# Stick-breaking attention: one split running sum instead of a separate sum of later blocks

## The reference, cut to what matters

```python
def stick_breaking(q, k, v, bias, qpos):
    kpos = jnp.arange(k.shape[1])
    z = (jnp.einsum('bqhd,bkhd->bhqk', q, k).astype(jnp.float32) * SB_SCALE
         + bias.astype(jnp.float32)[None, :, None, None])
    mask = kpos[None, :] < qpos[:, None]
    log_rest = jnp.where(mask, jax.nn.log_sigmoid(-z), 0.0)
    after = lax.cumsum(log_rest, axis=3, reverse=True) - log_rest
    a = jnp.where(mask, jnp.exp(jax.nn.log_sigmoid(z) + after), 0.0)
    return jnp.einsum('bhqk,bkhd->bqhd', a.astype(v.dtype), v)
```

## Time and profile before

| | us |
|---|---|
| median of 3 executions (1914.3 to 1914.96) | 1914.41 |
| the profiled execution | 1914.85 |
| its span, from first to last instruction | 1913.0 |
| TensorE busy | 1847.1 |
| VectorE busy | 834.4 |
| ScalarE busy | 542.8 |
| GpSimd busy | 305.3 |

### The profile page before, as it was taken

How to read it: one execution, slowest core, us unless ns; L and a number is a source line. 1 busy time by engine, 2 the same in 40 slices (tenths; PEclk the granted TensorE clock), 3 DMA queues, 4 the chain that set the end, 5 groups by cost and what they waited for, 6 DMA issues and landing times.

```text
span 1913.0 us, 28812 instructions
## 1 busy us (share of the span) xinstructions
PE 1847.1 (97%) x11073; PEld 1734.6 (91%) x11073; DVE 834.4 (44%) x1064; ACT 542.8 (28%) x871; POOL 305.3 (16%) x323
## 2 busy tenths in 40 slices
PE   6999999999899999999999989999999999999997
PEld 6878686968769989999999969999999999999996
DVE  5564737375812132232233385443124442344436
ACT  5564737372100010000022453332023220132213
POOL 1121313132501131111110121100001001010012
PEclk9999999999899999999999999999999999999998
DMA  5202030303331111111114031111111111111302
GB/s 162 67 24 66 1 88 0 87 2 110 105 115 44 40 43 38 55 50 39 49 51 143 23 112 55 44 45 54 44 44 44 47 45 48 47 44 45 135 29 94
DMA packets 162280, 113.69 MB, mean 59 GB/s; under 512 B 5389, under 2 KB 152213, under 8 KB 161947
## 3 DMA queue, kind: packets, MB, share of 16 engines
q1 hardware_dynamic: 161035, 108.34, 19.0%
q10 hardware_dynamic: 1200, 4.75, 0.7%
HBM read 95.86 MB, written 13.40 MB: 57 GB/s over the span
## 4 chain that ended last, share of the span: by engine, by line
PE 81%; DVE 11%; issue 3%; POOL 2%; ACT 2%; DMA 1%; SPq 0%; DVEq 0%; POOLq 0%; ACTq 0%
PE ps L1423 65%; PE ps L1433 8%; DVE zl L1105 2%; PE misc L1514 2%; POOL sp_hi L591 2%; PE misc L1409 1%; PE ps L1686 1%; PE ps L1504 1%; DVE kq L1145 1%; DVE later L1122 1%; DVE later L1118 1%; DVE sp_lo L1127 1%; DVE w_lo L1027 1%; DVE z_dec L1147 1%; PE ps L1499 1%
## 5 line engine op out<-in xcount | busy, mean ns | idle before, releaser
L1027 DVE TENSOR_TENSOR w_lo<-stage,w_hi 128x1024 fp32r<-128x1024 f32 x148 | 185.4, 1253 | 590.1 <-POOL w_hi L547 589.8
L1423 PE MATMUL ps<-h_hi,w_lo 128*128 128x344 f32 x1896 | 404.4, 322 | 0.0
L1423 PE MATMUL ps<-h_lo,w_hi 128*128 128x344 f32 x1896 | 403.2, 321 | 0.0
L1423 PE MATMUL ps<-h_hi,w_hi 128*128 128x344 f32 x1896 | 401.1, 320 | 0.0
L547 POOL TENSOR_SCALAR w_hi<-stage 128x1024 fp32r<-128x1024 f32 x148 | 158.0, 1068 | 1259.4 <-PE ps L1423 1097.4
L1423 PEld LDWEIGHTS ps<-h_lo,w_hi 128*128 128x128 f32 x1896 | 321.6, 189 | 0.0
L1423 PEld LDWEIGHTS ps<-h_hi,w_lo 128*128 128x128 f32 x1896 | 319.7, 188 | 1.8 <-issue 1.4
L1423 PEld LDWEIGHTS ps<-h_hi,w_hi 128*128 128x128 f32 x1896 | 316.7, 188 | 0.0
L1433 PE MATMUL ps<-h_hi,w_lo 128*128 128x344 f32 x408 | 147.7, 362 | 0.4 <-DVE w_lo L1027 0.4
L950 ACT ACTIVATE up<-ps 128x1032 f32<-128x1032 f32 x44 | 45.6, 1035 | 354.7 <-PE ps L1423 353.0
L1433 PE MATMUL ps<-h_hi,w_hi 128*128 128x344 f32 x408 | 134.5, 330 | 0.0
(11 more groups left out here) (257 smaller groups left out, 2558.3 us busy)
## 6 DMA issues: line engine op xcount, KB each, us to landing
stage<-in_w_in SPq DMA_DIRECT2D x48, 512.0 KB, 3.9
stage<-in_w_up SPq DMA_DIRECT2D x44, 512.0 KB, 3.8
stage<-in_w_down SPq DMA_DIRECT2D x16, 448.0 KB, 3.3
stage<-in_w_branch SPq DMA_DIRECT2D x24, 256.0 KB, 2.7
x_scratch<-trunk SPq DMA_DIRECT2D x1, 4128.0 KB, 13.9
x_back<-x_scratch SPq DMA_DIRECT2D x1, 4128.0 KB, 13.3
x_tok<-in_x_prompt SPq DMA_DIRECT2D x8, 512.0 KB, 8.4
kv_pg<-in_cache_k SPq DMA_DIRECT2D x16, 256.0 KB, 3.4
```

The lines of the kernel that those rows point to most:

```text
L1027: V.tensor_tensor(w_lo[par][:, :, :], stage[par][:, :, :], w_hi[par][:, :, :].bitcast(F32), ALU.subtract).then_inc(w_lo_made, 1)
L1423: last = M(ps[par][:, c, :], w[par][:, k, :], x[:, c * CH:(c + 1) * CH], start=(k == 0 and s == 0), stop=(k == n - 1 and s == 2))
```

## The change

For each chunk, own block and later blocks are now one running sum `sums` (softplus plus bias of this chunk, added to the sum of the chunk before). It is split into s_hi and s_lo. The sum within a block still takes neg_tri, now times the running sum of this chunk; the later blocks take `neg_rest`, which is minus one just where neg_tri is zero, times the running sum of the chunk before, as two float32r products. So GpSimd's high half waits for `sums_made` and not for `spn_ready`, every chunk has a sum (the `last` ones too), and the low half is a plain subtraction. ScalarE does abs, exp and ln of chunk c together, and its abs waits for the low half of chunk c - 4. The copies out of PSUM stand behind the low half of chunks 5, 13 and 22. GpSimd makes one more mask at the start, and the sample group's sums have one more product.

```diff
         ones = sb("ones", [P, P])
-        neg_ones = sb("neg_ones", [P, P])
         neg_tri = sb("neg_tri", [P, P], F32R)
+        neg_rest = sb("neg_rest", [P, P], F32R)
...
-        sp_hi = [sb(f"sp_hi{i}", [P, HALF], F32R, s_att) for i in range(3)]
-        sp_lo = [sb(f"sp_lo{i}", [P, HALF], F32R, s_att) for i in range(3)]
-        later = [sb(f"later{i}", [P, HALF], F32, s_att) for i in range(4)]
+        sums = [sb(f"sums{i}", [P, HALF], F32, s_att) for i in range(2)]
+        s_hi = [sb(f"s_hi{i}", [P, HALF], F32R, s_att) for i in range(4)]
+        s_lo = [sb(f"s_lo{i}", [P, HALF], F32R, s_att) for i in range(4)]
...
-            pool.wait_ge(consts, NCONST + 1)
+            pool.wait_ge(consts, NCONST + 3)
+            nc.gpsimd.affine_select(out=neg_rest[:, :], in_=neg_rest[:, :], compare_op=ALU.is_ge, fill=0.0,
+                                    base=-1, pattern=[[1, P]], channel_multiplier=-1).then_inc(consts, 1)
...
-                    pool.wait_ge(spn_ready, p * NCK + (c + 1))
+                    pool.wait_ge(sums_made, p * NSUMS + sums_upto[c + 1])
                     pool.wait_ge(cum_ready, p * NCK + (c + 1))
                     pool.sem_inc(hi_begun, 1)
-                    nc.gpsimd.tensor_scalar(sp_hi[c % 3][:, 0:W], zl[c % 4][:, 0:W], bias_p[:, hh:hh + 1], 1.0,
-                                            ALU.add, ALU.mult).then_inc(hi_ready, 1)
+                    nc.gpsimd.tensor_scalar(s_hi[c % 4][:, 0:W], sums[c % 2][:, 0:W], 1.0, 0.0,
+                                            ALU.mult, ALU.add).then_inc(hi_ready, 1)
...
                     act.wait_ge(z_ready, p * NCK + (c + 1))
-                    act.wait_ge(sp_ready, p * NCK + (c + 1))
+                    if c >= 4:
+                        act.wait_ge(sp_ready, p * NCK + c)
...
                     if c < NCK:
                         soft_abs(c)
-                    if 0 < c <= NCK:
-                        soft_ln(c - 1)
-                    if c < NCK:
                         soft_exp(c)
+                        soft_ln(c)
...
+                    t = zl[c % 4][:, 0:W]
+                    dve.wait_ge(l_ready, p * NCK + (c + 1))
+
+                    V.scalar_tensor_tensor(t, z_bank[c][:, 0:W], nbias_p[:, hh:hh + 1], t, ALU.max, ALU.add
+                                           ).then_inc(spn_ready, 1)
+
+                    dve.wait_ge(spn_ready, p * NCK + (c + 1))
+                    total = sums[c % 2]
+                    Wb = 0 if top else CHUNKS[c - 1][3]
+                    if Wb:
+                        dve.wait_ge(sums_made, p * NSUMS + sums_upto[c])
+                        V.scalar_tensor_tensor(total[:, W - Wb:W], t[:, W - Wb:W], bias_p[:, hh:hh + 1],
+                                               sums[(c - 1) % 2][:, 0:Wb], ALU.add, ALU.add).then_inc(sums_made, 1)
+                    if Wb < W:
+                        V.scalar_tensor_tensor(total[:, 0:W - Wb], t[:, 0:W - Wb], bias_p[:, hh:hh + 1],
+                                               ones[:, 0:W - Wb], ALU.add, ALU.mult).then_inc(sums_made, 1)
+                    dve.wait_ge(cum_ready, p * NCK + (c + 1))
+                    dve.wait_ge(hi_ready, p * NCK + (c + 1))
+                    V.tensor_tensor(s_lo[c % 4][:, 0:W], total[:, 0:W], s_hi[c % 4][:, 0:W].bitcast(F32),
+                                    ALU.subtract).then_inc(sp_ready, 1)
                     for j, (_, end) in enumerate(A_STEPS):
-                        if c == end - 1:
+                        if c == end:
...
-                    M(z, neg_tri[:, :], sp_lo[c % 3][:, 0:W], start=False, stop=False, skip_group_check=True)
-                    t = M(z, neg_tri[:, :], sp_hi[c % 3][:, 0:W], start=False, stop=top, skip_group_check=True)
+                    M(z, neg_tri[:, :], s_lo[c % 4][:, 0:W], start=False, stop=False, skip_group_check=True)
+                    t = M(z, neg_tri[:, :], s_hi[c % 4][:, 0:W], start=False, stop=top, skip_group_check=True)
                     if not top:
                         Wb = CHUNKS[c - 1][3]
-                        pe.wait_ge(later_ready, p * NLATER + later_upto[c])
-                        t = M(z[:, W - Wb:W], neg_ones[:, :], later[(c - 1) % 4][:, 0:Wb], start=False, stop=True,
+                        M(z[:, W - Wb:W], neg_rest[:, :], s_lo[(c - 1) % 4][:, 0:Wb], start=False, stop=False,
+                          skip_group_check=True)
+                        t = M(z[:, W - Wb:W], neg_rest[:, :], s_hi[(c - 1) % 4][:, 0:Wb], start=False, stop=True,
                               skip_group_check=True)
```

More of the change, by code:

```diff
@@ L112, in build @@
     NCK = len(CHUNKS)
[L114 to L118, removed]
+    sums_upto = [0]
+    for n, (_, _, _, W, top, _) in enumerate(CHUNKS):
+        sums_upto.append(sums_upto[-1] + 1 + (not top and W > CHUNKS[n - 1][3]))
+    NSUMS = sums_upto[NCK]
     SEGMENT_ENDS = [n for n, chunk in enumerate(CHUNKS) if chunk[5]]
@@ L320, in build @@
             ktok_ps, ktok_made, vtok_ps, vtok_made, small_ps, small_made, tok_out, z_ready,
-            abs_made, e_made, l_ready, spat_biased, q_pads, spn_ready, hi_ready, sp_ready, later_ready, cum_ready,
+            abs_made, e_made, l_ready, spat_biased, q_pads, spn_ready, hi_ready, sp_ready, sums_made, cum_ready,
             att_ready, pv_done, yc_hi_made, yc_made, pad_zero, own_mask, own_made, dec_o_ps, xg_ps,
@@ L336, in build @@
             "small_ps", "small_made", "tok_out", "z_ready", "abs_made", "e_made", "l_ready", "spat_biased", "q_pads",
-            "spn_ready", "hi_ready", "sp_ready", "later_ready", "cum_ready", "att_ready", "pv_done",
+            "spn_ready", "hi_ready", "sp_ready", "sums_made", "cum_ready", "att_ready", "pv_done",
             "yc_hi_made", "yc_made", "pad_zero", "own_mask", "own_made", "dec_o_ps", "xg_ps",
@@ L557, in _ @@
             nc.gpsimd.memset(ones[:, :], 1.0).then_inc(consts, 1)
-            nc.gpsimd.memset(neg_ones[:, :], -1.0).then_inc(consts, 1)
+            nc.gpsimd.memset(neg_rest[:, :].bitcast(F32), -1.0).then_inc(consts, 1)
             nc.gpsimd.memset(mask_b[:, :], NEG).then_inc(consts, 1)
@@ L565, in _ @@
                                     base=0, pattern=[[-1, P]], channel_multiplier=1).then_inc(consts, 1)
-            nc.gpsimd.affine_select(out=neg_tri[:, :], in_=neg_ones[:, :], compare_op=ALU.is_ge, fill=0.0,
+            nc.gpsimd.affine_select(out=neg_tri[:, :], in_=neg_rest[:, :], compare_op=ALU.is_ge, fill=0.0,
                                     base=0, pattern=[[-1, P]], channel_multiplier=1).then_inc(consts, 1)
@@ L662, in _ @@
             act.dma_start(g_pre[:, :], norm_mix_pre[0, :].partition_broadcast(P)).then_inc(gpre_in, 16)
-            act.wait_ge(consts, NCONST + 4)
+            act.wait_ge(consts, NCONST + 5)
             for b in range(len(IN_BATCHES) + 1):
@@ L1074, in _ @@
                 dve.wait_ge(biasp_made, p * 2 + 2)
-                nl = 0
                 def segment_lo(n):
@@ L1101, in _ @@
                                 V.tensor_copy(a_tail[:, :], last_cols(1, PTAIL)).then_inc(tail_cols, 1)
[L1102 to L1130, removed]
                 segment_lo(NSEG - 2)
@@ L1177, in _ @@
             V.tensor_tensor(zf, dec_sums, zf, ALU.add).then_inc(dec_arg, 1)
-            dve.wait_ge(consts, NCONST + 4)
+            dve.wait_ge(consts, NCONST + 5)
             V.tensor_reduce(pick[:, :], ident[0:NS * H, 0:NS * H].rearrange("p (h b) -> p b h", h=H), AX_X, ALU.add
@@ L1438, in _ @@
             ys = [(y_hi[:, k, :], y_lo[:, k, :]) for k in range(BT)]
-            pe.wait_ge(consts, NCONST + 4)
+            pe.wait_ge(consts, NCONST + 5)
             FIRST_Q = {4: (0, 0, KT), 5: (0, KT, KT), 6: (0, 2 * KT, KT),
@@ L1629, in _ @@
             M(dec_sums, neg_tri[:, :].bitcast(F32), sp_d, start=True, stop=False, skip_group_check=True)
-            M(dec_sums[:, 0:half], neg_ones[:, :], sp_d[:, half:], start=False, stop=True, skip_group_check=True
-              ).then_inc(dec_cum, 1)
+            M(dec_sums[:, 0:half], neg_tri[:, :].bitcast(F32), sp_d[:, half:], start=False, stop=False,
+              skip_group_check=True)
+            M(dec_sums[:, 0:half], neg_rest[:, :].bitcast(F32), sp_d[:, half:], start=False, stop=True,
+              skip_group_check=True).then_inc(dec_cum, 1)
             for g in range(SG):
```

## The result

| | before | after |
|---|---|---|
| median of 3 executions, us | 1914.41 | 1961.33 (1960.49 to 1967.43) |
| the profiled execution | 1914.85 | 1960.49 |
| its span | 1913.0 | 1958.6 |

The changed kernel is slower: its time is 1.0248 of the time before, with a 95% interval of 1.0230 to 1.0265. The forecast was 1958 us.

A forecast was written before the change was run, and what follows sets the result against it. VectorE's lengthened rounds in the attention stage were taken as the bound, with TensorE waiting. 1914.85 + 35.7 (8.9 a pass) + 8.0 (clock) + 0.2 = 1958.8, corrected to the median: 1958 us, range 1928 to 1975.

The forecast's parts named there:

- TensorE's saving is lost: Attention stage: TensorE's heavy step of 2.87 us lies under VectorE's 3.16, so 21 us saved count only behind the last wait.
- the signs named: Attention passes: TensorE waits for the low half in nearly every chunk, and 4 to 6 us before the transposes of a_tail.
- The rival at 1893: Attention stage: TensorE is the bound and its 21 us saving counts; needs a high half under 0.40; chance 0.08.
- The round: VectorE's 512-column chunk: softplus, sum, GpSimd's high half (0.69, as measured alone) and low half in sequence, 3.16 us against 2.88.
- The 0.55: Low bound for GpSimd's 512-column high half: 1.20 less its overlap with `later`; with no clock loss it gives 1941 us.
- upper figure of 1975: Total time if the low half takes 0.67 and each hand-over 0.1 more, given as 22 us a pass.
- the transposes of a_tail: End of a pass, TensorE: they start at 70.3 instead of 60.87, 9.4 later, because the copies stand behind chunk 22's low half.
- The rival at 1929: End of a pass: it does not end on the a_tail copy; 3.5 us a pass, no clock loss; chance 0.07.
- The clock: TensorE behind the a_tail wait: 5.1 us at half speed, 2.0 us a pass, 8 us in all, bounds 0 and 10.4.
- costs nothing: ScalarE's new order: abs, exp, ln and weights of a chunk take under 3.0 us, below VectorE's 3.16.
- the lead pays nothing further: ScalarE's earlier ln: with VectorE slowest, its input for chunks 2 to 23 is already there, so no gain.
- has its next three scores by then: Chunk 13: TensorE waits some 3 us for an a_raw copy, hidden because VectorE already has its next three scores.

The follow-up runs named there:

- e1: The changed kernel with all three copies out of PSUM, and a_tail's, put ahead of the softplus of chunks 4, 12 and 21 again: 1941.47 us, 1.0129.
- e5: The changed kernel without the product of s_lo and neg_rest, so the weights leave out the low half of the later blocks: 1959.11 us, 1.0219.
- e11: The changed kernel with only the third a_raw copy and a_tail's ahead of the softplus of chunk 21, the other two left late: 1942.59 us, 1.0142.
- e4: The changed kernel with ScalarE's old order, abs of chunk c, ln of c - 1, exp of c: 1977.17 us, 1.0322.
- e9: The changed kernel with the low half of chunk c - 1 between softplus and sum of c, weight split and copies behind the sum: 1894.16 us, 0.9886.
- e8: The changed kernel with the copies early and the high half taken by VectorE itself instead of GpSimd: 1899.77 us, 0.9915.

## Why the prediction was right

- **The bound.** The step that TensorE's saving is lost because VectorE's round (3.16) lies above TensorE's step (2.87) held. TensorE's busy time in the page is 11.8 us less, not the 21 of the forecast; in e1, which lacks the stretches at the lower clock, it is 15.0 less. e5 shows that 14 us of TensorE's work can be left out with little or no effect. Two of the signs named were not quite met: TensorE waits for the low half in about 11 of the 24 chunks of a pass (33 waits in three passes), not in nearly every one, and the wait before the transposes is 3.88 us, not 4 to 6. The rival at 1893 fell on the point named for it: the high half would have had to be under 0.40 and is 0.62.
- **The round.** Forecast 0.87 + 0.75 + 0.22 + 0.69 + 0.03 + 0.60 = 3.16; measured 0.87 + 0.75 + 0.26 + 0.62 + 0.11 + 0.61 = 3.22 (201.09 to 204.31). Two terms were off in opposite directions: the high half was 0.07 shorter than the 0.69 I took, and the two hand-overs together 0.12 longer. The other rounds are 3.35, 2.84, 2.35 (each 0.04 or 0.05 over the forecast) and 1.61 (1.58). The 0.07 is the same at every width (0.37 and 0.30 for 128 columns, 0.69 and 0.62 for 512), and the two instructions differ: the old one adds `bias_p`, a value per partition, and the new one has only constants. That this is the 0.07 is likely but not tested. The 0.55 was no duration alone: the same instruction that took 1.20 beside `later` took 0.69 alone in the kernel before, so the overlap of 0.65 had cost it 0.51 and not the whole 0.65. The prediction's upper figure of 1975 is 1973 by its own terms (22 x 0.17 x 4 on 1958).
- **The rank of the terms.** The forecast put 9.4 of its 10.9 us a pass on one event, the transposes of a_tail. The end of the pass on VectorE and then on TensorE, beside the earlier trace rows:

```profile
254.20 1.31 DVE L1109 TENSOR_TENSOR s_lo<-sums,s_hi 128x384 fp32r<-128x384 f32 x1 [0.89 <-POOL s_hi L592]
255.44 0.50 DVE L1117 COPY a_raw<-ps 128x344 f32 x1
255.86 0.17 DVE L1120 COPY a_tail<-ps 128x23 f32<-128x23 f32 x1
```

```profile
256.08 0.27 PE L1399 MATMUL ps<-ident,q_dec 128*8 128x128 f32 x1 [3.88 <-DVE a_tail L1120]
```

  The pass starts at 184.67 (chunk 0's scores), so the transposes come 71.4 into it, where 70.3 was forecast and 60.87 was the time before. Chunks 1 to 22 are 61.5 instead of 60.3 without VectorE's other work: that is all of the difference, and it is the hand-overs (22 x 0.12 = 2.6) less the shorter high half (22 x 0.07 = 1.5).
- **The two causes in it.** e1 and e11 split the 11.3. With a_tail early the pass is 108.3 us, so 4.8 is the place of the copies and the clock behind the wait, and 6.5 is the longer round. The rival at 1929 was wrong about the changed kernel, whose pass does end on a_tail. e1 is the kernel that it describes, and there it is wrong in size: 3.5 us a pass against 6.5. Both it and the prediction let TensorE take up chunk 20's sum as soon as its low half is there, at 63.7. TensorE in the changed kernel, at the sums of chunks 19 and 20:

```profile
248.01 0.50 PE L1489 MATMUL ps<-s_lo,neg_tri 128*128 128x512 f32 x1 [0.26 <-DVE s_lo L1109]
...
250.88 0.30 PE L1489 MATMUL ps<-s_lo,neg_tri 128*128 128x128 f32 x1
```

  The last wait is the one for chunk 19's low half. TensorE has 2.87 us of work from there to chunk 20's sum and comes to it at 66.2 (250.88), though VectorE had the low half at 64.9. The wait before the transposes is shorter by this than the forecast's 5.5.
- **The clock: mis-sized.** The forecast took 5.1 us at the lower level and 2.0 us lost a pass. TensorE in windows of 2 us in the changed kernel (window, busy, granted clock, DMA), beside the earlier trace rows:

```profile
253.00:255.00 2.00, 0.00 (x0) 1.00 0.00 0
255.00:257.00 2.00, 0.92 (x9) 0.97 0.00 0
257.00:259.00 2.00, 2.00 (x9) 0.50 0.02 5
259.00:261.00 2.00, 2.00 (x11) 0.68 0.04 7
261.00:263.00 2.00, 2.00 (x14) 1.00 0.78 211
```

  The clock is at the upper level while TensorE waits, falls to 1.2 GHz at about 256.9, 0.8 us after it has begun again, and is back at 260.3. Products of 344 columns are 0.288 apart there and 0.158 before and after. The stretch is 3.4 us, as it is in the other three passes, and what lies behind the transposes has grown from 16.8 to 17.5 us in all where +1.5 was forecast. With the 0.5 that the last two sums save the clock is worth about 1.2. It shows in the 24 projection products of one step, which take 5.17 us (257.36 to 262.53) and took 3.86 before. The mechanism was right; the size came from the place of the earlier trace rows. There the clock had fallen while TensorE still waited (the granted clock is 0.81 from 500 to 501, so it fell at about 500.6) and stayed low until 507.4, 5.1 us behind the wait.
- **What cancelled.** +1.1 for the rounds and -0.8 for the clock leave 11.2 against 10.9 a pass (11.3 measured). The closeness of 1958 to 1961 is partly luck, since the +1.1 is itself 2.6 less 1.5, though each of the two terms was right within 1.1 us.
- **ScalarE.** That the order "costs nothing" and "the lead pays nothing further" holds for the changed kernel, but the reason was incomplete. The new order is what lets TensorE's wait at chunk 13 pass without harm; e4 prices the order at 16 us in all, and 2.12 of the 4.3 us of the pass that was followed are this wait. I looked for that wait at VectorE only ("has its next three scores by then") and didn't ask through which ScalarE queue those scores reach it.

## What to carry to other kernels

When two engines pass a value back and forth in each round, add up the round of the chain before the work of any engine: an operation that was hidden beside the helper's costs its whole length once it must come first, even when the helper gets faster by it. Delay the step that needs the helper's answer by one operation of the next round (e9), or let the first engine do the small operation itself (e8). And give each item behind a wait its own question: the copies of a_raw and a_tail behind chunk 22, 0.6 us together, cost 20 us because TensorE's next work waited for them behind two engines' rounds, while a copy of the same loop behind chunk 13 cost nothing, as long as ScalarE's order kept VectorE fed.

## What the runs showed of the hardware that I hadn't expected

- A hand-over from VectorE to GpSimd took 0.26 us (202.71 to 202.97) and back 0.11 (203.59 to 203.70). In e8 a VectorE instruction that depends on the one before starts 0.03 to 0.04 behind its end (186.84 to 186.87, 187.62 to 187.66); in the changed kernel the sum starts 0.13 behind the softplus (201.83 to 201.96).
- VectorE takes the high half of 512 columns in 0.43 (e8) where its operations with two tensor inputs take 0.69 to 0.75 for the same width. GpSimd takes 0.30, 0.41, 0.52 and 0.62 for 128, 256, 384 and 512 columns alone. Its old high half, with `bias_p`, took 0.69 for 512 alone and 1.20 beside a VectorE operation.
- A wait of 3.88 us on TensorE cost only about 1.2 us more in clock. In the four passes the lower level lasted 3.4 us each time and began 0 to 1.3 us after the work had begun again (pass 1: 144.2 against 143.0; pass 4: both at 482.2). At the earlier trace rows, behind a wait of 3.68, it began during the wait.
